# From the third step on, a gated layer's weight blocks stand still in TensorE and the tokens stream past: what becomes of the time

## What is computed

```
def _rmsnorm(x, g):
    xf = x.astype(jnp.float32)
    y = xf * lax.rsqrt(jnp.mean(xf * xf, axis=-1, keepdims=True) + EPS)
    return (y * g.astype(jnp.float32)).astype(x.dtype)

def _swiglu(x, w_in, w_out):
    gate, up = jnp.split(x @ w_in, 2, axis=-1)
    return (jax.nn.silu(gate) * up) @ w_out
...
    x = x + 0.5 * _swiglu(_rmsnorm(x, n1_g[l]), ffn1_w_in[l], ffn1_w_out[l])
...
    x = x + 0.5 * _swiglu(_rmsnorm(x, n3_g[l]), ffn2_w_in[l], ffn2_w_out[l])
```

## Time and profile before

| | us |
|---|---|
| median of three runs | 1760.0 |
| runs | 1758.71, 1760.12, 1760.0 |
| profiled execution, its own time | 1760.5 |
| span of its trace | 1758.5 |
| TensorE (PE) busy | 1741.8 |
| VectorE (DVE) busy | 1113.5 |
| ScalarE (ACT) busy | 1047.4 |
| GpSimd (POOL) busy | 157.2 |

### The profile page before, as it was taken

How to read it: one execution, slowest core, us unless ns; L and a number is a source line. 1 busy time by engine, 2 the same in 40 slices (tenths; PEclk the granted TensorE clock), 3 DMA queues, 4 the chain that set the end, 5 groups by cost and what they waited for, 6 DMA issues and landing times.

```text
span 1758.5 us, 22044 instructions
## 1 busy us (share of the span) xinstructions
PE 1741.8 (99%) x8381; PEld 1428.2 (81%) x8381; DVE 1113.5 (63%) x1578; ACT 1047.4 (60%) x1646; POOL 157.2 (9%) x137
## 2 busy tenths in 40 slices
PE   8999999999999999999999999999999999999998
PEld 7888887688888877888888888888888888778887
DVE  6756567677665777754477745387775447776543
ACT  7655567757665766655475754377665447666452
POOL 0000011500000010200000200002020000102000
PEclk9999999999999999999999999999999999999999
DMA  8554454254554633555444554453455445335551
GB/s 316 208 182 182 170 189 144 96 192 176 207 188 150 224 120 121 203 192 183 176 185 172 219 184 179 165 204 144 156 203 183 179 175 194 129 111 204 191 191 72
DMA packets 44905, 310.36 MB, mean 176 GB/s; under 512 B 5232, under 2 KB 5616, under 8 KB 8320
## 3 DMA queue, kind: packets, MB, share of 16 engines
q1 hardware_dynamic: 44384, 307.79, 47.5%
q0 software_dynamic: 272, 1.05, 0.2%
q10 hardware_dynamic: 144, 0.11, 0.0%
HBM read 307.88 MB, written 1.05 MB: 176 GB/s over the span
## 4 chain that ended last, share of the span: by engine, by line
PE 96%; DVE 1%; DMA 1%; POOL 1%; ACT 1%; issue 0%; SPq 0%; DVEq 0%; ACTq 0%
PE ps L1963 29%; PE ps L1965 29%; PE ps L1964 29%; PE ps L2034 2%; PE ps L2138 1%; DMA raw<-in_w_parts 1%; POOL proj L1895 1%; PE ps L2403 1%; PE ps L2389 1%; PE ps L2417 1%; PE ps L2375 0%; PE ps L2226 0%; DVE wlo L1186 0%; PE ps L2405 0%; PE ps L2643 0%; PE ps L2219 0%
## 5 line engine op out<-in xcount | busy, mean ns | idle before, releaser
L1963 PE MATMUL ps<-whi,xhi 128*128 128x512 f32 x1568 | 628.4, 401 | 0.6 <-DVE wlo L1186 0.5
L1965 PE MATMUL ps<-whi,xlo 128*128 128x512 f32 x1568 | 612.5, 391 | 0.0
L1964 PE MATMUL ps<-wlo,xhi 128*128 128x512 f32 x1568 | 611.3, 390 | 0.0
L1186 DVE SCALAR_TENSOR_TENSOR wlo<-raw,first,whi 128x512 fp32r<-128x512 f32 x704 | 493.9, 763 | 156.7 <-ACT whi L639 156.3
L639 ACT ACTIVATE whi<-raw,first 128x512 fp32r<-128x512 f32 x704 | 449.7, 713 | 139.4 <-PE ps L1965 117.3
L1183 DVE TENSOR_TENSOR wlo<-raw,whi 128x2048 fp32r<-128x2048 f32 x110 | 251.5, 2290 | 172.7 <-ACT whi L634 172.7
L1963 PEld LDWEIGHTS ps<-whi,xhi 128*128 128x128 f32 x1568 | 294.8, 188 | 63.1 <-issue 4.5
L1965 PEld LDWEIGHTS ps<-whi,xlo 128*128 128x128 f32 x1568 | 294.4, 188 | 62.9
L1964 PEld LDWEIGHTS ps<-wlo,xhi 128*128 128x128 f32 x1568 | 295.2, 188 | 55.5
L634 ACT ACTIVATE whi<-raw 128x2048 fp32r<-128x2048 f32 x110 | 210.2, 1915 | 131.1 <-PE ps L1965 87.3
L1963 PE MATMUL ps<-whi,hhi 128*128 128x512 f32 x720 | 283.4, 394 | 0.9 <-DVE hlo L1314 0.9
(11 more groups left out here) (220 smaller groups left out, 1065.2 us busy)
## 6 DMA issues: line engine op xcount, KB each, us to landing
raw<-in_w_parts SPq DMA_DIRECT2D x285, 1024.0 KB, 4.8
gain<-in_gains SPq DMA_DIRECT2D x10, 512.0 KB, 6.3
x<-in_x SPq DMA_DIRECT2D x2, 512.0 KB, 6.7
raw<-in_w_parts SPq DMA_DIRECT2D x2, 512.0 KB, 6.0
arena<-in_bias_line POOLq DMA_DIRECT2D x1, 1024.0 KB, 11.4
out<-x SPq DMA_DIRECT2D x4, 256.0 KB, 2.0
const<-in_const_in SPq DMA_DIRECT2D x1, 288.0 KB, 13.2
proj<-in_suffix_in SPq DMA_DIRECT2D x1, 128.0 KB, 13.1
```

The lines of the kernel that those rows point to most:

```text
L1186: nc.vector.scalar_tensor_tensor(out=lo[:, cols], in0=whole[:, cols], scalar=gcol[:, COLUMNS[n] + kk:COLUMNS[n] + kk + 1], in1=hi[:, cols] ...
L1963: nc.tensor.matmul(out_ap, a_hi, wh, start=first, stop=False)
L1964: nc.tensor.matmul(out_ap, a_hi, wl, start=False, stop=False)
L1965: return nc.tensor.matmul(out_ap, a_lo, wh, start=False, stop=last)
```

## The change

From step 2 on, a gated layer's `up` is done by `up_turned(i, j, u)`: for each panel of part j, blocks of 128 weight columns stand in the array (u = 0: the two gate blocks, u = 1: the two up blocks), and the tokens stream past. With a block of `whi`, upper and lower x go through together as 512 columns (they now lie side by side in `xs`); with the block of `wlo`, upper x alone, 256 columns. The result has hidden columns on partitions, so that h needs no transpose. In its bank the left 256 columns hold upper by upper and lower by upper, the right 256 columns upper by lower; ScalarE copies the right half out (`gated_copy`) and VectorE adds the left (`gated_sum`). The row scale, now along the free axis, is a row broadcast over partitions by two small matmuls (`rows_of_scales`, then the copy `ROW`). GpSimd, idle in these layers before, multiplies twice (`gated`). Steps 0 and 1 stay as they were; their four transposed tiles now go to banks 0 to 3. `up_turned` uses all of banks 4 to 7 in every step.

```diff
+TURNED_KINDS = ("gated",)
...
-        xhi = sb("xhi", [P, KT, SEQ], F32R)
-        xlo = sb("xlo", [P, KT, SEQ], F32R)
+        xs = sb("xs", [P, KT, 2, SEQ], F32R)
+        xhi, xlo = xs[:, :, 0, :], xs[:, :, 1, :]
...
+        ROW = proj[:, 1, 4608:4608 + SEQ]
+        HHI_T = hhi[:].rearrange("p t k n -> p k t n")
+        HLO_T = hlo[:].rearrange("p t k n -> p k t n")
+        G_PART = [proj[:, 0, BANK * u:BANK * (u + 1)].rearrange("p (m n) -> p m n", m=2) for u in range(2)]
+        G_SCALED, G_SIG = [proj[:, 0, BANK * u:BANK * (u + 1)].rearrange("p (m n) -> p m n", m=2) for u in (2, 3)]
...
+        def hidden_bank(s, i, t):
+
+            return 2 * i + t if s["kind"] in TURNED_KINDS else 6 + t
...
+        def turned_banks(u, lower):
+
+            return ps[:, 4 + 2 * u:6 + 2 * u, SEQ * lower:SEQ * (lower + 1)]
...
+                def gated_copy(i, u):
+                    act.wait_ge(job_done, s["n_job"] + nth_job(i, u))
+                    if i >= 3:
+                        if u == 0:
+                            act.wait_ge(gscaled_ready, gated_count(s, i - 1))
+                        else:
+                            act.wait_ge(gh_ready, gated_count(s, i - 1))
+                    nc.scalar.activation(G_PART[u], turned_banks(u, 1), ACT.Copy).then_inc(gcopy_ready, 1)
+
+                def gated_sigmoid(i, step_of):
+                    if step_of == 0:
+                        act.wait_ge(gscaled_ready, gated_count(s, i))
+                        if i >= 3:
+                            act.wait_ge(gh_ready, gated_count(s, i - 1))
+                        step(nc.scalar.activation(G_SIG, G_SCALED, ACT.Exp, scale=-1.0))
+                    elif step_of == 1:
+                        step(nc.scalar.activation(G_SIG, G_SIG, ACT.Ln, bias=1.0))
+                    else:
+                        nc.scalar.activation(G_SIG, G_SIG, ACT.Exp, scale=-1.0).then_inc(gsig_ready, 1)
+
+                def gated_hidden_hi(i):
+                    act.wait_ge(gh_ready, gated_count(s, i))
+                    if i >= 4:
+                        wait_freed(act, place["down", i - 4][-1])
+                    nc.scalar.activation(HHI_T[:, hidden_slots(s, i), :, :], turned_h(i, 0), ACT.Copy).then_inc(ghi_ready, 1)
+
...
+                if kind_turned:
+                    act.wait_ge(row_ps, s["n_rows"] + 1)
+                    nc.scalar.activation(ROW, ps[:, 3, 0:SEQ], ACT.Copy).then_inc(row_ready, 1)
+                if kind_turned and gated:
+                    for i in range(2, iters):
+                        after = place["down", i - 2][-1] + 1
+                        if i == 2:
+                            for j, t in ((0, 0), (0, 1), (1, 0)):
+                                hidden_hi(j, t)
+                            hi_to(after + 1)
+                            hidden_hi(1, 1)
+                            hi_to(after + 2)
+                        else:
+                            hi_to(after + 2)
+                            gated_hidden_hi(i - 1)
+                        hi_to(after + 3)
+                        gated_copy(i, 0)
+                        gated_sigmoid(i, 0)
+                        gated_copy(i, 1)
+                        gated_sigmoid(i, 1)
+                        gated_sigmoid(i, 2)
+                    gated_hidden_hi(iters - 1)
+                if kind_turned:
+                    return
                 for i in range(2, iters):
                     after = place["down", i - 2][-1] + 1
...
+                def gated_sum(i, u):
+                    dve.wait_ge(gcopy_ready, 2 * gated_count(s, i) - 1 + u)
+                    nc.vector.tensor_tensor(G_PART[u], turned_banks(u, 0), G_PART[u], ALU.add).then_inc(gsum_ready, 1)
+
+                def gated_scale(i):
+                    dve.wait_ge(gsum_ready, 2 * gated_count(s, i) - 1)
+                    dve.wait_ge(row_ready, s["n_rows"] + 1)
+                    if i >= 3:
+                        dve.wait_ge(gswish_ready, gated_count(s, i - 1))
+                    nc.vector.tensor_tensor(G_SCALED, G_PART[0], ROW.unsqueeze(1).to_broadcast([P, 2, SEQ]), ALU.mult
+                                            ).then_inc(gscaled_ready, 1)
+
+                def gated_product(i):
+                    dve.wait_ge(gup_ready, gated_count(s, i))
+                    dve.wait_ge(gswish_ready, gated_count(s, i))
+                    if i < 4:
+                        for t in range(NT):
+                            dve.wait_ge(ht_ready, it0 + NT * (i - 2) + t + 1)
+                    else:
+                        dve.wait_ge(glo_ready, gated_count(s, i - 2))
+                    nc.vector.tensor_tensor(H[i % 2][:, 0, :].rearrange("p (m n) -> p m n", m=2), G_SIG, G_PART[1], ALU.mult
+                                            ).then_inc(gh_ready, 1)
+
+                def gated_hidden_lo(i):
+                    dve.wait_ge(ghi_ready, gated_count(s, i))
+                    slots = hidden_slots(s, i)
+                    nc.vector.tensor_tensor(HLO_T[:, slots, :, :], turned_h(i, 0), HHI_T[:, slots, :, :].bitcast(F32),
+                                            ALU.subtract).then_inc(glo_ready, 1)
...
+                if kind_turned and gated:
+                    for i in range(2, iters):
+                        after = place["down", i - 2][-1] + 1
+                        if i == 2:
+                            for j, t in ((0, 0), (0, 1), (1, 0)):
+                                hidden_lo(j, t)
+                            lo_to(after + 1)
+                            hidden_lo(1, 1)
+                            lo_to(after + 2)
+                        else:
+                            lo_to(after + 1)
+                            gated_product(i - 1)
+                            lo_to(after + 2)
+                            gated_hidden_lo(i - 1)
+                        lo_to(after + 3)
+                        gated_sum(i, 0)
+                        gated_scale(i)
+                        gated_sum(i, 1)
+                    gated_product(iters - 1)
+                    gated_hidden_lo(iters - 1)
+                    return
                 for i in range(2, iters):
                     after = place["down", i - 2][-1] + 1
                     lo_to(after + (0 if gated and i == 2 else 2 if gated else 1))
...
+            def gated(s):
+                for i in range(2, s["iters"]):
+                    pool.wait_ge(gsum_ready, 2 * gated_count(s, i))
+                    pool.wait_ge(row_ready, s["n_rows"] + 1)
+                    nc.gpsimd.tensor_tensor(G_PART[1], G_PART[1], ROW.unsqueeze(1).to_broadcast([P, 2, SEQ]), ALU.mult
+                                            ).then_inc(gup_ready, 1)
+                    pool.wait_ge(gsig_ready, gated_count(s, i))
+                    nc.gpsimd.tensor_tensor(G_SIG, G_SIG, G_SCALED, ALU.mult).then_inc(gswish_ready, 1)
...
+                def rows_of_scales():
+
+                    pe.wait_ge(norm_ready, s["norms"])
+                    for t in range(NT):
+                        ins = nc.tensor.matmul(ps[:, 3, t * P:(t + 1) * P],
+                                               stat[:, RS, ROW_NORM + t:ROW_NORM + t + 1].to_broadcast([P, P]), ident,
+                                               start=True, stop=True)
+                    ins.then_inc(row_ps, 1)
+
...
+                def up_turned(i, j, u):
+
+                    n = place["up", i][j]
+                    if j == 0 and i == 2:
+                        for t in range(NT):
+                            pe.wait_ge(act_ready, act0 + nth_job(u, t))
+                    elif j == 0:
+                        pe.wait_ge(gsum_ready, 2 * gated_count(s, i - 1) - 1 + u)
+                    for kk in range(PANELS):
+                        k = PANELS * j + kk
+                        if u == 0:
+                            weights(n, kk)
+                        for m in (2 * u, 2 * u + 1):
+                            cols = slice(kk * BANK + m * P, kk * BANK + (m + 1) * P)
+                            nc.tensor.matmul(ps[:, 4 + m, :], whi[n % HIS][:, cols], xs[:, k, :, :].rearrange("p h n -> p (h n)"),
+                                             start=(k == 0), stop=False)
+                            ins = nc.tensor.matmul(ps[:, 4 + m, 0:SEQ], wlo[n % LOS][:, cols], xhi[:, k, :], start=False,
+                                                   stop=(k == KT - 1))
+                    if j == 1:
+                        ins.then_inc(job_done, 1)
+                    elif u == 1:
+                        ins.then_inc(w_used, 1)
+
+                def hidden_ready(i, t):
...
+                if kind_turned:
+                    rows_of_scales()
+                    for i in range(2, iters):
+                        if i == 2:
+                            for j in range(2):
+                                up_turned(2, j, 0)
+                            for h, t in ((0, 0), (0, 1), (1, 0)):
```

(14 more changed lines are left out.)

57 lines of the change are left out of this document (45 added, 12 removed).

## The result

The changed kernel takes 1773.7 us (median of 4 runs, 1772.05 to 1775.61), the kernel before 1759.4 on the same chip (4 runs, 1758.28 to 1760.12). The ratio is 1.0084, with a 95% interval of 1.0071 to 1.0096: 14.3 us slower. The prediction said 1767 (1758 to 1773): the direction was right, the size was not, and the time lies 0.7 us outside the range.

A forecast was written before the change was run, and what follows sets the result against it. The prediction took TensorE's stream and its waits to bound the kernel. Its terms, 3.3 - 8.4 + 5.0 + 3.9 + 0.2 + 0.6 + 1.9, sum to +6.5 us on 1760.5, giving 1767 (range 1758 to 1773).

The forecast's parts named there:

- Term 1: Turned `up` panels: 4 wide and 4 narrow matmuls take 1.383 us instead of 1.360; +3.3 us over 144 panels.
- Term 2: Transposes of steps 2 to 10 go in both gated layers, 0.47 us a group: -8.4 us.
- Terms 3, 4 and 7: TensorE waits at the entry of step 2 (+5.0 us), at down(0) (+3.9 and +0.2), behind the second gated layer (+1.9).
- Term 5: Steady steps of the gated layers: 16.5 us each, with no wait for the other engines, cost 0.
- Term 6: End of each gated layer: TensorE waits 1.05 us for step 10's h; net of earlier idle times, +0.6 us.
- The clock: Rival: TensorE's clock falls at the new waits, each of four adding up to 1.7 us: 1768.5 to 1774; chance 0.2.

The follow-up runs named there:

- second try: Changed kernel with h(0, 1) and down(0)'s split moved earlier, the next part's split after the last lower h, last up scale on VectorE: 1760.15 us.
- runs of eight: On the second try, eight 512-column matmuls of a part and half, then its eight 256-column ones, instead of by turns: 1757.2 us.
- Twos: Changed kernel with each panel's two wide matmuls together, then its two narrow ones, instead of by turns: 1770.8 us.
- all narrow: On the second try, each 512-column turned matmul split into two of 256 columns, each with its own load: 1763.4 us.
- edits of the order alone: Changed kernel with one reordering each: h(0, 1) before the next split, 1768.6 us; down(0)'s split earlier, 1770.6; next stage's split earlier, 1778.2.
- 384 or 512 columns: Changed kernel with the lower weight blocks meeting 384 or 512 columns of x instead of 256: 1802.2 and 1827.3 us.
- edit of down(0): Changed kernel with the split of down(0)'s part moved ahead of the copies of h on ScalarE and VectorE: 1770.6 us.
- third edit alone: Changed kernel with only the split of the next stage's second part moved ahead of the last product: 1778.2 us, ratio 1.0114.

## Why the prediction came out as it did

- **Bound on TensorE's stream and its waits**: right. Removing waits, and with them the falls of the clock behind them, brought 1773.7 to 1760.15.
- **Term 1, streaming**: this is the step that failed, as a size. The prediction took "119, near the measured row" for a narrow matmul and 226.7 for the wide one beside it, from rows in which each width stood among its own kind. A narrow one takes up to 120, and the wide ones behind it are slower by 9: a pair is 352.8 ns and not 345.7, +7.4 us in `up` and +1.0 in `down` instead of +3.3. That wide ones could lose by their neighbours had no place in the sum. The trace of the kernel before shows it: in the step of the earlier trace rows the second to sixth wide ones behind the four transposes stand 231, 235, 229, 232 and 231 ns apart and the next 227, some 25 ns lost, a part of the 0.47 that the prediction read as the transposes' own price. And the sentence that no 256-column matmul with 128 stationary columns is in that trace holds for fp32r only: there are 32 of plain float32 operands (1227.79 us and on), 216 ns apart, no guide to this price.
- **Term 2, transposes**: -8.4, right. The second try, without waits, gives back the time of before: +7.4 and +1.0 against -8.4.
- **Terms 3, 4 and 7**: 5.2, 4.2 and 1.9 against 5.0, 4.1 and 1.9, and each wait went away when what was named as its cause was moved. Shown.
- **Term 5, steady steps**: no wait in them, right; their length was given as 16.5 us and is 16.8, by term 1 alone.
- **Term 6**: 0.9 against 0.6. The lateness after was priced right: 0.91 and 1.20 us in the two layers, 2.1 as forecast. That of before was put at 1.5 and is 1.2, by the starts. In these two places GpSimd's operations take 1.29 to 1.30 us each and not the 1.41 taken.
- **The clock**: the prediction held it at 0.2 that falls come with the new waits, at up to 1.7 us each. The profiled execution had two more than before, +3.3. It isn't the same in each execution: the four of the changed kernel took 1772.05, 1773.65, 1773.72 and 1775.61, steps of about 1.6 to 1.9, and the eleven of runs of eight 1755.66 to 1756.02 or 1757.22 to 1757.76. That these steps are one fall each fits the price and the mean clocks (0.996 at 1775.61, 0.999 at 1772.05); for executions without a trace it is argued, not shown.

Against the median: 14.3 measured. Without the clock the table sums to 12.2, 5.7 above the forecast, and 5.1 of that is term 1. The other 2.1 are about one more fall of the clock. Both misses point the same way, and the range had room for the clock or for the stream, not for both.

The Trainium skill (TensorE: Matmul & The Clock Gate, Back-to-back issue gap) has N/2.4 + 2.5 ns for the gap, 109 ns at 256 columns; it calls that the gap of a single matmul and not that of a stream in which each has its load. With a load for every matmul it is 120 here among narrow ones and 127 beside wide ones, so no measurement agrees. By the page's figures the prediction's term 1 would be +0.7 us, not the +0.8 it states; nothing hangs on it.

**A version that beats both.** Runs of eight with all waits gone is 2.6 us faster than the kernel before by the medians (1757.2 against 1759.8 there), 0.15%, interval 0.06% to 0.24%: real by its interval, but under the 0.2% that was set as telling from no change. Twos instead of runs of eight would be as good by these figures: 1760.15 less the 3.3 that twos gave, some 1756.9. That is an estimate; no run has twos with all waits gone.

## What to carry to other kernels

A duration read where an instruction stands among its own kind is not its price beside another kind: look for a mixed row (here the wide matmuls behind the transposes), or hold the sum open by what the neighbours may lose. If TensorE must stream two widths with a weight load each, put them in twos or longer runs, not by turns; longer runs than two brought nothing more. And when a job is made to use all banks at once, everything that was ready a job later becomes due now: reorder the other engines' lists for it, and ask of each moved split which chain it now stands in.

## What was not expected of the hardware

- **A debt behind narrow matmuls.** Narrow matmuls (256 columns, a 128 x 128 load each) run at 120 ns, and five 512-column ones behind them are 1 to 9 ns late each, some 26 ns in all, after 8 narrow ones as after 96, and much the same behind four transposes. By turns it adds up to 63 ns. What holds it isn't visible. The loads don't run further ahead and lose their lead: in the traces of both kernels, of twos, of runs of eight and of all narrow, a load starts 2 to 5 ns after the start of the matmul before its own, at any width, as long as nothing waits. It is recorded with 187 to 192 ns, so a matmul behind a narrow one starts some 74 ns before its load ends and one behind a wide one 35 ns or more after, and the second to fifth wide ones are late all the same.
- **The clock and the length of a wait.** 2.72 us without a start (the GpSimd wait) was followed by a fall to 0.50 in the kernel before, in each of the edits of the order alone and in runs of eight, and by none in the changed kernel, with 384 or 512 columns, in the second try and all narrow (one profiled execution each). 2.1 us before down(0) brought one in the second layer of the changed kernel and none in the first; the 2.27 us before step 2 brought one in both layers of the changed kernel, in the second alone with the edit of down(0), and in neither with the third edit alone. Each stretch lasted 3.4 us but one of 6.8 (third edit alone, behind the second layer's end). What decides stays open.
- **VectorE and GpSimd beside each other.** The groups of GpSimd's two multiplications in the changed kernel:

```profile
L2033 POOL TENSOR_TENSOR proj<-proj 128x512 f32<-128x512 f32 x18 | 29.7, 1648 | 0.0
...
L2030 POOL TENSOR_TENSOR proj<-proj 128x512 f32<-128x512 f32 x18 | 23.4, 1298 | 345.7 <-DVE proj L1430 345.7
```

The same work on 128 x 512 floats takes 1.30 us, and in 14 of the 18 steps of the second multiplication 1.73 to 1.76. In each of these 14 it starts while VectorE is in a panel of its split of `w_in` and ends 1.15 to 1.16 us after that panel does; the next panel, begun beside it, is recorded with 1.78 us instead of 0.74 and ends 0.55 us after GpSimd's operation. So the two do not slow each other evenly: they look like taking turns, an operation each. That is also how three panels come to 3.11 us above, beside a GpSimd operation of 1.75, where eight took 5.38. It cost nothing here, since steady steps have slack, but it stretches a chain that ends in a wait.
